# Routing weight and gate applied as the expert output leaves PSUM, and a residual of two additions in the last stage

## What is computed

```
f = sum over the 2 chosen experts e of  w[t,e] * (silu(u @ Wg[e]) * (u @ Wu[e])) @ Wd[e]
x = LayerNorm(ALPHA * x + gate2 * f) * ln2_g + ln2_b       # gate2: one row of 1024, for all tokens
```

## Time and profile before

| | us |
|---|---|
| median of 3 runs (767.47 to 769.25) | 768.04 |
| the profiled execution | 767.53 |
| its span in the trace | 765.4 |
| routing stage, last output product to first block product | 418 to 457 |
| blocks, first product to last | 457 to 723 |
| gathers, residual, second norm, stores | 724 to 765 |

### The profile page before, as it was taken

The page is one execution under the profiler, slowest core; times in us unless marked ns, Lnnn a source line. Parts: engine busy times, 40 slices in busy tenths (PEclk is TensorE's granted clock), DMA queues, the critical chain, the costliest instruction groups (busy, mean ns, idle before and its releaser), DMA issues.

```text
span 765.4 us, 15490 instructions
## 1 busy us (share of the span) xinstructions
PE 647.1 (85%) x5985; PEld 424.4 (55%) x5986; DVE 344.2 (45%) x657; ACT 250.9 (33%) x522; POOL 98.2 (13%) x185
## 2 busy tenths in 40 slices
PE   0799999998989799999999339899999999999700
PEld 0275666676767577777787224455555545555400
DVE  0265444478888775585675653111111101111058
ACT  0234434557444564465401201111111111111144
POOL 0131000200000000000000032122222212222140
PEclk9999999999999899999999559999999999999955
DMA  9999767292311322213881998999999999961162
GB/s 298 373 313 308 249 220 238 105 314 79 111 44 41 99 66 82 83 56 111 296 363 74 393 419 316 421 418 418 420 419 419 418 419 420 418 261 41 48 219 110
DMA packets 83874, 189.78 MB, mean 248 GB/s; under 512 B 7384, under 2 KB 59832, under 8 KB 68480
## 3 DMA queue, kind: packets, MB, share of 16 engines
q1 hardware_dynamic: 67616, 149.05, 51.7%
q0 software_dynamic: 7376, 32.26, 11.9%
q10 hardware_dynamic: 8848, 8.01, 3.2%
HBM read 175.23 MB, written 14.07 MB: 247 GB/s over the span
## 4 chain that ended last, share of the span: by engine, by line
PE 63%; DMA 12%; DVE 12%; ACT 6%; issue 4%; SPq 2%; ACTq 0%; POOL 0%; POOLq 0%; DVEq 0%
PE psum L1485 17%; PE psum L1496 9%; DMA raw<-in_w_in_dram 7%; PE psum L1293 6%; PE psum L1295 6%; PE psum L1294 6%; DMA wu<-in_moe_w_up_dram 3%; PE psum L1414 2%; PE psum L1416 2%; PE psum L1415 2%; PE psum L1468 2%; PE psum L1259 2%; PE psum L1475 2%; SPq L398 1%; PE psum L1336 1%
## 5 line engine op out<-in xcount | busy, mean ns | idle before, releaser
L1485 PE MATMUL psum<-wg,xs 128*32 128x256 f32 x1280 | 149.8, 386 | 3.8 <-issue 2.1
L1485 PE MATMUL psum<-wu,xs 128*32 128x256 f32 x1280 | 149.2, 386 | 0.0
L1293 PE MATMUL psum<-uh,whi 128*128 128x512 f32 x336 | 137.9, 410 | 1.7 <-DVE wlo L875 1.7
L1295 PE MATMUL psum<-uh,wlo 128*128 128x512 f32 x336 | 131.3, 391 | 0.0
L1294 PE MATMUL psum<-ul,whi 128*128 128x512 f32 x336 | 131.3, 391 | 0.0
L1485 PEld LDWEIGHTS psum<-wg,xs 128*32 128x32 f32 x1280 | 73.0, 111 | 57.1 <-issue 5.5
L1192 DVE TENSOR_TENSOR h_sb<-psum,hsil 64x256 f32<-64x256 f32 x40 | 17.1, 427 | 151.8 <-ACT hsil L784 151.8
L875 DVE TENSOR_TENSOR wlo<-raw,whi 128x1024 fp32r<-128x1024 f32 x42 | 51.4, 1224 | 68.7 <-ACT whi L611 68.5
L1496 PE MATMUL psum<-wd,hT 128*32 128x256 f32 x1280 | 77.4, 382 | 0.4 <-DVE hT L1196 0.4
L1293 PEld LDWEIGHTS psum<-uh,whi 128*128 128x128 f32 x336 | 63.3, 189 | 23.4 <-issue 7.4
L1485 PEld LDWEIGHTS psum<-wu,xs 128*32 128x32 f32 x1280 | 72.0, 111 | 0.0
(11 more groups left out here) (258 smaller groups left out, 842.7 us busy)
## 6 DMA issues: line engine op xcount, KB each, us to landing
wg<-in_moe_w_gate_dram SPq DMA_DIRECT2D x32, 1024.0 KB
wu<-in_moe_w_up_dram SPq DMA_DIRECT2D x32, 1024.0 KB
wd<-in_moe_w_down_dram SPq DMA_DIRECT2D x32, 1024.0 KB
raw<-in_w_in_dram SPq DMA_DIRECT2D x42, 512.0 KB, 3.9
ada<-in_ada_w_dram POOLq DMA_DIRECT2D x16, 1024.0 KB, 5.2
ada<-in_ada_w_dram SPq DMA_DIRECT2D x8, 1024.0 KB, 17.1
y_d<-ysb ACTq DMA_DIRECT2D x160, 32.0 KB
y_d<-zrow POOLq DMA_DIRECT2D x8, 512.0 KB, 6.4
```

The source lines that it names most:

```text
L1293: mmul(bank[s % 2], h[:, k, :], uh[:, k, :], start=(k == 0), stop=False)
L1295: ins = mmul(bank[s % 2], l[:, k, :], uh[:, k, :], start=False, stop=(k == KT - 1))
L1485: ins = mmul(psum[32 * g:32 * g + 32, 0, 0:256], xs[:, k % 2, k // 2, :], wgu[slot][g // 2][:, k, (g % 2) * 256:(g % 2) * 256 + 256], star ...
```

## The change

The weight and gate2 are applied block by block. Behind the `idx` product, VectorE makes eight further one-hot matrices `at_w` (block, times the token's normalised weight `wtok`), TensorE multiplies them with `at_pos` (`slot_weights`, fp32), and VectorE copies the result to `wcol`, one weight per slot and block. gate2 is loaded as `gate2c`, [128, 256], in the layout of `bank[3]`, by four DMAs where `gate2r`, [128, 1024], took one. VectorE empties `bank[3]` with one `scalar_tensor_tensor` (`y_weighted`: bank times weight column times gate2c), and ScalarE is left with the four stores (`y_store`). VectorE's loop over blocks is unrolled by four, as ScalarE's was. In the last stage `weigh` is gone, VectorE waits for the gathers itself, and `residual` is an addition and a `tensor_tensor_reduce`, which adds `x1` and sums the row. ScalarE's pass for the row sum is gone, and the root is called once on a spare tile ahead of the stage. The loads of ln2's rows wait for `wcol_ps` where they waited for `idx_ps`.

```
-            sp.dma_start(gate2r[:, :], row_of(2)).then_inc(rows_in, 16)
+            for g in range(4):
+                sp.dma_start(gate2c[32 * g:32 * g + 32, :],
+                             mod_flat[2 * D + 256 * g:2 * D + 256 * g + 256].partition_broadcast(32)).then_inc(ln1_in, 16)
...
-            sp.wait_ge(S["idx_ps"], 1)
+            sp.wait_ge(S["wcol_ps"], 1)
...
-            def y_out(b, q, stored):
-
-                act.wait_ge(S["d_ps"], b + 1)
-                act.wait_ge(y_st[q], stored)
-                A(ysb[q][:, :], bank[3][:, 0:256], ACT.Copy).then_inc(S["y_ev"], 1)
+            def y_store(b, q):
+
                 act.wait_ge(S["y_ev"], b + 2)
...
-            def weigh(t):
-                act.wait_ge(fgather[t], 32)
-                A(fin[t][1][:, :], fin[t][1][:, :], ACT.Copy, scale=wA[:, t:t + 1]).then_inc(S["fin_a"], 1)
...
-                A(spare, z, ACT.Copy, accum_out=fsum[:, t, 0:1]).then_inc(S["fin_s"], 1)
-                act.wait_ge(S["fin_s"], 3 * t + 1)
                 A(fsum[:, t, 1:2], fsum[:, t, 0:1], ACT.Copy, scale=-1.0 / D).then_inc(S["fin_s"], 1)
...
+            A(tiny[:, 1, :], tiny[:, 1, :], ACT.Sqrt).then_inc(S["rt_exp"], 1)
...
-            mark(V.tensor_tensor(wA[:, :], wr[:, 0, :], wsum[:, :], ALU.mult))
-            mark(V.tensor_tensor(wB[:, :], wr[:, 1, :], wsum[:, :], ALU.mult))
+            mark(V.tensor_tensor(wtok[:, :, :], wr[:, :, :], wsum[:, :].unsqueeze(1).to_broadcast([P, 2, NT]), ALU.mult))
...
+            for t in range(NT):
+                for r in range(2):
+                    V.tensor_scalar(at_w[:, r, t, :], iota[:, 0:TCOL], fr[:, r, t:t + 1], wtok[:, r, t:t + 1],
+                                    ALU.is_equal, ALU.mult).then_inc(S["slotw"], 1)
...
+            dve.wait_ge(S["wcol_ps"], 1)
+            chain(V.tensor_copy(wcol[:, 0:TCOL], bank[7][:, 256:256 + TCOL]))
...
+            def y_weighted(b, q, stored):
+                dve.wait_ge(S["d_ps"], b + 1)
+                dve.wait_ge(y_st[q], stored)
+                V.scalar_tensor_tensor(ysb[q][:, :], bank[3][:, 0:256], wcol[:, bass.ds(b, 1)], gate2c[:, :],
+                                       ALU.mult, ALU.mult).then_inc(S["y_ev"], 1)
...
-            with dve.Fori(NT, nblk) as b:
-                h_columns(b - 1)
-                gate_times_up(b)
-            h_columns(nblk - 1)
+            with dve.Fori(NT, nblk, 4) as b:
+                for j in range(4):
+                    h_columns(b + (j - 1))
+                    gate_times_up(b + j)
+                    if j == 0:
+                        y_weighted(b - 1, 3, b * 16)
+                    else:
+                        y_weighted(b + (j - 1), j - 1, b * 16 + 64)
+            more_quads = last // 4
+            h_columns(more_quads * 4 + 3)
+            y_weighted(more_quads * 4 + 3, 3, more_quads * 64 + 64)
...
-                dve.wait_ge(S["fin_a"], t + 1)
-                chain(V.scalar_tensor_tensor(z[:, :], yb_[:, :], wB[:, t:t + 1], ya_[:, :], ALU.mult, ALU.add))
-                chain(V.tensor_tensor(z[:, :], z[:, :], gate2r[:, :], ALU.mult))
-                V.tensor_tensor(z[:, :], z[:, :], x1[:, t, :], ALU.add).then_inc(S["fin_z"], 1)
+                dve.wait_ge(fgather[t], 32)
+                chain(V.tensor_tensor(z[:, :], ya_[:, :], yb_[:, :], ALU.add))
+                V.tensor_tensor_reduce(z[:, :], z[:, :], x1[:, t, :], 1.0, 0.0, ALU.add, ALU.add, fsum[:, t, 0:1])\
+                    .then_inc(S["fin_z"], 1)
...
+            def slot_weights():
+
+                for t in range(NT):
+                    for r in range(2):
+                        pe.wait_ge(S["slotw"], 2 * t + r + 1)
+                        ins = mmul(bank[7][:, 256:256 + TCOL], at_pos[:, r, t, :].bitcast(F32), at_w[:, r, t, :],
+                                   start=(t == 0 and r == 0), stop=(t == NT - 1 and r == 1), skip_group_check=True)
+                ins.then_inc(S["wcol_ps"], 1)
```

More of the change, by code:

```diff
@@ L173, in hybrid_layer @@
         epst = small("epst", [P, 1])
-        wA = small("wA", [P, NT])
-        wB = small("wB", [P, NT])
         yrow = small("yrow", [P, 2, NT], U32)
@@ L301, in hybrid_layer @@
         at_blk = route("at_blk", [P, 2, NT, TCOL], F32R)
+        at_w = route("at_w", [P, 2, NT, TCOL])
+        wtok = route("wtok", [P, 2, NT])
         assert route.at <= R_A + 16 * KB, route.at - R_A
@@ L320, in hybrid_layer @@
         ysb = [at(R_W + 32 * KB + KB * i, f"ysb{i}", [P, 256])[0] for i in range(4)]
-        gate2r, o = at(o, "gate2r", [P, D])
+        gate2c, o = at(o, "gate2c", [P, 256])
+        wcol, o = at(o, "wcol", [P, 64])
         g1r, o = at(o, "g1r", [P, D])
@@ L1210, in _ @@
             for b in range(1, NT):
[L1211 removed]
+                h_columns(b - 1, again=b > 1)
                 settle(b)
                 gate_times_up(b)
+                y_weighted(b - 1, b - 1, 64)
             nblk = dve.value_load(ctrl[0:1, NUM:NUM + 1], min_val=NE, max_val=NBLK)
[L1215 to L1220 removed]
+            last = dve.value_load(ctrl[0:1, LAST + NE - 1:LAST + NE], min_val=NE - 1, max_val=NBLK - 1)
+            with dve.Fori(NT, nblk, 4) as b:
[9 more added lines that the diff above has]
+            y_weighted(more_quads * 4 + 3, 3, more_quads * 64 + 64)
+            dve.wait_ge(rows_in, 16 * 5)
             dve.wait_ge(S["x1_done"], NT)
@@ L1528, in _ @@
             pe.wait_ge(S["d_ps"], nblk)
-            for done in ("gu_ps", "xT_m_ps", "d_ps"):
+            for done in ("gu_ps", "xT_m_ps", "hT_ps", "d_ps"):
                 pe.sem_inc(S[done], 3)
```

35 lines of the change are left out of this document (16 added, 19 removed).

## The result

| | before | after |
|---|---|---|
| median, us | 767.94 (767.47 to 769.25, 4 runs) | 761.5 (760.73 to 762.93, 4 runs) |
| ratio after to before | | 0.9918, 95% interval 0.9902 to 0.9934 |
| the profiled execution, us | 767.53 | 761.0 |
| its span, us | 765.4 | 759.0 |

The changed kernel is faster by 0.8%, 6.4 us. The forecast was 762.2, in a range of 759.8 to 765.0.

What follows compares the result with a forecast made beforehand. TensorE was taken to bound the blocks and DVE the last stage. Last stage -6.05, end of blocks +0.35 and routing +0.15 gave -5.55 us, forecast 762.2, range 759.8 to 765.0.

Steps and rivals of the forecast that it cites:

- The last stage, -6.05: Last stage: from tile 0's gathers landing to DVE's end, 22.16 us instead of 28.21, a gain of 6.05.
- the lower bound that I had named: Last stage: the reduce costs a plain pass, 1.22 us, with no write of the sum; gain then 6.7 us.
- The rival of half speed: Last stage: the reduce takes 2.61 us, gain 1.7 less 0.5, about 766.6 us; chance 0.10.
- The end of the blocks, +0.35: Hand-over to the last stage: DVE's evacuation delays the last hT copy and down; 0.35 us added, bounds 0.1 to 1.0.
- Inside the blocks, nothing: Blocks: the hT copy some 0.25 us later is covered, since down runs 3.6 us after it; no cost.
- Routing, +0.15: Routing stage: 0.07 us gained ahead of idx, 0.2 lost by GpSimd copies meeting DVE's passes; together +0.15.
- the two named copies: Routing stage: GpSimd's copies of the first index and xgs, now beside DVE work; 0 to 0.6 us, taken as 0.2.
- The clock rival: First block: extra TensorE passes raise the clock from 0.50 to 1.00, saving up to 1.6 us, 760.6; chance 0.13.
- Late gathers: Last stage: GpSimd's last gathers slowed beside DVE's additions; DVE waits 2 to 3 us if tile 2 is late, 764.8; chance 0.05.
- The sum: Whole kernel: -6.05 + 0.35 + 0.15 = -5.55 us, span from 765.4 to 759.85, profiled execution to 762.0.

Runs made afterwards that it cites:

- the second execution of the same kernel: The changed kernel timed once more, unedited, against the kernel before: 762.85 us, ratio 0.9922.
- the evacuation alone: Kernel before, with DVE instead of ACT emptying bank 3 by a plain copy, loop unrolled by four, last stage unchanged: 768.51 us, ratio 1.0002.
- the run with the settling moved: Changed kernel with DVE's settling of x1's first tile moved behind the first gate_times_up: 760.94 us, ratio 0.9918.
- The filler runs: Changed kernel plus two or three fp32 128x512 products on TensorE ahead of the first block: 761.95 us (0.992) and 760.74 us (0.991).
- the additions on GpSimd: Changed kernel with GpSimd instead of DVE adding the gathered tiles 2 and 3: 763.3 us, ratio 0.9933.
- the last stage alone: Kernel before with the changed kernel's last stage; weights and gate2 applied nowhere: 759.8 us, ratio 0.9881.
- hT first: Changed kernel with DVE copying hT of a block before emptying bank 3 of the block before: 761.42 us, ratio 0.9905.

## Why the prediction was right, and where it was off

**The last stage, -6.05: right in kind, 1.1 too small.** The mis-sized term is the reduce. I took 1.28 and 0.16 for the pass and its write; measured are 1.23 and 0.08. A residual costs 2.41 (742.89 to 745.30) instead of 2.72, because the next instruction starts 1.15 behind the start of the pass plus the 0.08. Three residuals that count give 0.93, and tile 1 landed 0.17 earlier relative to tile 0 than counted. That is the difference between 22.16 and 21.03. The 0.93 holds in every execution; the 0.17 is luck, since in the second execution of the same kernel tile 1 landed 0.08 later than counted, and the stretch is 21.28. The case lies at the lower bound that I had named (1.22 and no write). `normalise` was 2.72, and is 2.71.

**The rival of half speed fell.** A sum costs the pass nothing: 1.23 with it, 1.22 without. The Trainium skill's sentence on the `scalar_tensor_tensor` family with two SBUF sources that aren't bf16 ("Vector Engine (DVE) Microarchitecture Reference", "Points that are easy to get wrong") would give 2.5, an estimate: twice 1.22 to 1.28. This instruction, with two fp32 SBUF sources and an accumulated sum, shows none of it. The profile names it CUSTOM_DVE_ANT_0, so it need not be of that family; a `scalar_tensor_tensor` with a sum was not run.

**The end of the blocks, +0.35: right**, 0.34 in the table and 0.33 from L1499 to the evacuation's end, from +0.20 for `hT` and `down` and the rest for the evacuation of 0.48 instead of 0.38 and its start. In other executions with this end it is 0.48, and 0.62 with the evacuation alone, all inside the stated 0.1 to 1.0. What I had not named is that `down` waits for the evacuation too. It did not matter in this order, where the evacuation is done first, and it decides in the other.

**Inside the blocks, nothing: right.** A block takes 6.20 in every run, before and after, and the run with the evacuation alone isolates it.

**Routing, +0.15: the size came out, its terms did not.** From `idx` to `xs` it is +0.15 in this pair; to the first silu it is +0.35, but the rest is 0.06 ahead of `idx` and 0.14 in the first block's products, both of the size by which like executions differ. The mechanism was the one named, GpSimd's copies beside DVE's passes. Only one of the two named copies met one: `xgs`, 0.38 slower, and the run with the settling moved gives that back; the first index copy took 0.18, as before. What the prediction left out is the relief, that the second index copy and both gather issues are no longer beside DVE's passes, which let `xgs` start 0.17 earlier. That the two make 0.15 is luck.

**The clock rival** did not come about: 0.50 from 457 to 460. The filler runs show how near it was.

**Late gathers** were harmless: the seventh, beside DVE's first addition, took 1.36 instead of 0.94 (in the kernel before it was the eighth, with 1.45), and nobody waited for it. The mechanism is real, as the additions on GpSimd show.

**The sum**: -5.55 forecast, -6.41 measured in the span. The two differences, -1.14 and +0.20, and 0.09 spread over the blocks make up the 0.86. The profiled execution was forecast at 762.0 and is 761.0. The second set of runs has its median at 762.85; the forecast lies between the two. So how near the total came, 0.7 us, says little, since two sets of runs of one kernel differ by 1.35; what bears the prediction out is the last stage's 7 us, instruction by instruction.

**What stays open.** TensorE stands still for 4.26 us at 483.81 in after, where before it had 0.44 and 2.13 at that place, with no wait in the trace that explains it. The block 3 to 4 distance is 12.15 instead of 11.10. With the evacuation alone and with the last stage alone the stands are 0.49 and 1.37, and 0.44 and 1.63, and the distance is 8.69 and 8.90; in all eleven executions with the new routing the distance is 11.64 or more. So neither of these two parts makes it longer by itself; whether the rest of the change does was not tried. Little of it reaches the end, since block 25 waits for weights, whose transfers keep the DMA engines at a share of 1.02: the chain shows 25.28 us of such a transfer ahead of it, and block 25 comes 6.91 behind its predecessor instead of 8.03. From silu 0 to 25 it is 166.5 to 167.4 us in all runs but one (168.3, with hT first). Nor is the long store issue explained. The rows are of the chain of after:

```profile
483.81 4.26 issue
...
602.40 25.28 DMA wu<-in_moe_w_up_dram
```

## What to carry to other kernels

Carry elementwise work from the stage that an engine bounds to one where that engine idles, and check at the last iteration, where the cover ends: here 40 evacuations on DVE cost 0.3 to 0.5 us in all, and one DVE pass fewer per tile in the last stage, with the waits for ACT gone, gave 7. Before reordering work in front of a waiting engine, list all its waits: the profile names one of them, and not always the one that came last. Count GpSimd's elementwise work as DVE's where DVE's passes read two SBUF tiles. And before a mark in a trace is compared between two kernels, see how far it moves where the kernels do the same: here 2 us for the start of the blocks.

## What the runs showed of the hardware

- `tensor_tensor_reduce` on two fp32 SBUF tiles of 128x1024 takes 1.23 us, and the write of its sum 0.08, beside the next instruction; a plain addition takes 1.22. I had expected the sum to cost more.
- GpSimd and DVE slow each other. GpSimd's copy of 128x256 went from 0.40 to 0.78 us and ended 0.27 behind DVE's pass, its issue of a gather went from 0.94 to 1.36, and DVE's passes with two SBUF tiles from 1.28 and 1.22 to 3.25 and 3.35 beside an addition on GpSimd of 3.1. I had expected GpSimd alone to pay.
- TensorE's first products went from 0.64 to 0.41 and 0.39 us (granted clock 0.50 and 1.00) when 5.11 us of filler, behind 3.65 of slot products, led up to the transposes with no gap, and not with 3.74 us of filler and a gap of 0.79.
- One issue of a store on ACT's queue took 1.18 to 1.50 us instead of 0.32 in four of fourteen executions; nothing in their traces explains it but the one more packet on the instruction queue beside it.
